# Order of the three product terms inside a k tile: by token half instead of alternating halves

## The chip, the cores and the metric

The kernel runs on one core of one Trainium2 chip. The metric is the device time of one execution in microseconds; the time before is 1610.29 us, the median of three runs (1606.36, 1610.29 and 1698.71).

## The reference

One step of a two-layer decoder trunk in float32 on 576 tokens: a prompt of 512 and 8 x 8 sample tokens, model width 1024. Layer 0 mixes tokens with a chunked gMLP (width 3072), layer 1 with a recurrent block (RG-LRU, width 1024); a SwiGLU block (inner width 2816) follows each, and every block sits between two RMS norms. Nearly all of the arithmetic is in dense products:

```python
def gmlp_mixer(h, ...):
    z = gelu(h @ w_in + b_in); u, v = split(z)
    v = layer_norm(v); mixed = causal product of w_s with v, in chunks of 128
    return (u * mixed) @ w_out, v
def rglru_mixer(h, ...):
    y_br, x_br = split(h @ w_in)
    ... conv, gates, scan over tokens ...
    return (hs * gelu(y_br)) @ w_out
def swiglu(h, w_in, w_out):
    g, u = split(h @ w_in)
    return (silu(g) * u) @ w_out
x = x + rms_norm(mixer(rms_norm(x)));  x = x + rms_norm(swiglu(rms_norm(x)))
```

## The kernel before

Activations lie transposed: features on the 128 partitions, the 576 tokens along the free axis. The tokens are cut into two halves of 288 (HT), so that a half's sums fit one PSUM bank. A unit is one tile of 128 output features: its two halves take banks 2m and 2m+1, the pair m of four pairs.

Each float32 operand is split in two parts of a narrower format: activations into `hh` (high) and `hl` (low), weights into `whi` and `wlo`. A product then takes three matmuls for each k tile (128 input features) and each half: high weights with `hh`, high weights with `hl`, low weights with `hh`. The dropped fourth term is low times low. TensorE therefore runs 6 matmuls of 128 x 288 per k tile and unit, all issued by the helper `mm` (line 455), so every row of these matmuls bears line 455.

The stages, in order: V (the gMLP's v, lines 524 to 580, tokens as output rows, 384 columns wide), U (`u_body`, line 592, 24 units of 8 k tiles, with the chunk mixing between units), and then the phases GO, FI0, FO0, RI, RO, FI1, FO1. The FI phases and RI are units of 8 k tiles (`tile_unit`, line 718) behind an opening part (`first_tiles`, line 667). GO, FO0, RO and FO1 are `out_phase` (line 626): two groups G of 512 output features, each with four pairs open at once and the k tiles in the outer loop.

Two helpers set the order of the six matmuls. `three` (line 457) alternates the halves: bank a, bank b, for each of the three terms. It serves U, RI's and the FI phases' units behind the opening part, and in `out_phase` all k tiles but the last four of each group. `one_half` (line 467) does the three terms of one half, all into one bank. It serves the last four k tiles of each group of `out_phase` (for all of half 0 first, then half 1, lines 648 to 665) and all of `first_tiles`. Over the whole kernel `three` issues 1152 matmuls in U, 480 in each group of GO, 1920 in each FI phase, 432 in each group of FO0 and FO1, 576 in RI and 96 in each group of RO: 8448 in all. `one_half` issues 192 in each of the four out phases and 192 in each of the three opening parts: 1344.

Round TensorE: SP loads weights into four slots of `stage`; ScalarE rounds them to `whi` (line 800), VectorE subtracts to `wlo` (line 1109), and both wait for the unit that used the slot before. ScalarE and VectorE read finished pairs out of PSUM. A unit's only signal, `unit_done`, sits on the last matmul that the last call of `three` returns, the second half's low-weight term; in the last unit of U and of each FI phase every second k tile's last matmul also counts `h_pair_used` up.

Of the kernel before, what the change touches and what calls it, by code (L numbers as in the profile page):

```python
# [38 lines left out]
def trunk_kernel(nc, x_prompt, x_sample, state_conv, state_h, norm_gains,  # L39
# [7 lines left out]
    TT = T + TS  # L47
    HT = TT // 2
# [26 lines left out]
    with ExitStack() as ctx:  # L75
        def sb(name, shape, dt=F32):
            return ctx.enter_context(nc.sbuf_tensor(name, shape, dt))
# [6 lines left out]
        hh = sb("hh", [P, KD, TT], F32R)  # L84
        hl = sb("hl", [P, KD, TT], F32R)
# [34 lines left out]
        ps = ctx.enter_context(nc.psum_tensor("ps", [P, 8, BANK], F32))  # L120
# [18 lines left out]
        def half(h):  # L139
            return slice(h * HT, (h + 1) * HT)  # L140
# [63 lines left out]
        def xc(h):  # L204
            return wide[:, XC0 + h * TT:XC0 + (h + 1) * TT]
# [4 lines left out]
        def wg(mat, h):  # L210
            return wide[:, WG0 + (mat * KD + h) * P:WG0 + (mat * KD + h + 1) * P]
# [137 lines left out]
        def out_bank(b):  # L349
            return ps[0:P if PIECES[b][1] < NC else TS, OUT_BANK[b], :]  # L350
# [102 lines left out]
        def _(pe):  # L453
            def mm(out, w, x, start, stop):
                return pe.matmul(out, w, x, start=start, stop=stop)  # L455

            def three(m, hi_w, lo_w, k, first, last):

                a, b = ps[:, 2 * m, 0:HT], ps[:, 2 * m + 1, 0:HT]
                mm(a, hi_w, hh[:, k, 0:HT], first, False)  # L460
                mm(b, hi_w, hh[:, k, HT:TT], first, False)
                mm(a, hi_w, hl[:, k, 0:HT], False, False)
                mm(b, hi_w, hl[:, k, HT:TT], False, False)
                mm(a, lo_w, hh[:, k, 0:HT], False, last)
                return mm(b, lo_w, hh[:, k, HT:TT], False, last)

            def one_half(m, h, hi_w, lo_w, k, first, last):

                o = ps[:, 2 * m + h, 0:HT]
                mm(o, hi_w, hh[:, k, half(h)], first, False)  # L470
                mm(o, hi_w, hl[:, k, half(h)], False, False)
                return mm(o, lo_w, hh[:, k, half(h)], False, last)
# [34 lines left out]
            for k in range(KD):  # L507
                last = pe.transpose(ps[:, 7, k * TS:(k + 1) * TS], xin[NC][:, k * P:(k + 1) * P], ident[0:TS, 0:TS])
# [56 lines left out]
            for g in range(GRP):  # L565
                at = 4 * BANK + BANK + g * P if g < 4 else 6 * BANK + g * P - 4 * P
                last = pe.transpose(psf[:, at:at + P], wraw[:, g, :], ident[:, :])
# [7 lines left out]
            for k in range(KD):  # L575
                last = pe.transpose(ps[:, 5, 64 + 32 * k:96 + 32 * k], sraw[:, k * P:(k + 1) * P], ident[0:32, 0:32])
# [15 lines left out]
            def u_body(i, first=False, last_body=False):  # L592
                for c in range(6):
                    n = base["U"] + c
                    m = c % 3
                    pe.wait_ge(lo_ready, i * 6 + (n + 1))
                    if first and c < 3:
                        pe.wait_ge(z_evicted, NT * (GRP - 1) + min(2 * c + 2, NT))
                    else:
                        pe.wait_ge(pair_free[m], i * 2 + (c // 3))  # L600
                    for k in range(KD):
                        if last_body and c == 5 and k in (2, 5):
                            mix(i * 6 + 3 + k // 5, k // 5, 1, i * 2 + 1)
                        at = three(m, whi[:, slot(n), k * P:(k + 1) * P], wlo[:, slot(n), k * P:(k + 1) * P],
                                   k, k == 0, k == KD - 1)
                        if last_body and c == 5 and k % 2 and k < KD - 1:
                            at.then_inc(h_pair_used, 1)
                    at.then_inc(unit_done, 1)
                    if first and c < 2 or last_body and c == 5:
                        continue  # L610
                    if c % 3 == 2:

                        pe.wait_ge(ln_done, i * (2 * NT) + (c // 3 + 1) * NT)
                    gshift, f = divmod(c - 2, 3)
                    if first and c == 2:
                        pe.wait_ge(blk_landed, 16 * NB)
                        pe.wait_ge(rb_ready, 1)
                    mix(i * 6 + (c - 2), f, gshift % 2, i * 2 + gshift)
# [7 lines left out]
            def out_phase(name):  # L626
# [8 lines left out]
                for G in range(2):  # L635
                    first = base[name] + G * per
                    for j in range(per - 2):
                        pe.wait_ge(lo_ready, first + j + 1)
                        pe.wait_ge(a_lo, G * per + AB[name] + j + 1)
                        for kk in range(units[j][1]):  # L640
                            for m in range(4):
                                if j == 0 and kk == 0:
                                    pe.wait_ge(pair_free[m], G + free0[name][m])
                                last = three(m, *weights(first + j, kk, m), 2 * (j % 4) + kk, j == 0 and kk == 0, False)
                        last.then_inc(unit_done, 1)
# [72 lines left out]
            def tile_unit(n, m, freed, last_unit, i=0, per=0):  # L718
                pe.wait_ge(lo_ready, i * per + (n + 1))
                pe.wait_ge(pair_free[m], freed)  # L720
                for k in range(KD):
                    last = three(m, whi[:, slot(n), k * P:(k + 1) * P], wlo[:, slot(n), k * P:(k + 1) * P],
                                 k, k == 0, k == KD - 1)
                    if last_unit and k % 2 and k < KD - 1:
                        last.then_inc(h_pair_used, 1)
                last.then_inc(unit_done, 1)
# [21 lines left out]
            for mat in range(2):  # L748
                for h in range(KD):
# [3 lines left out]
                    for b in range(2):  # L753
                        last = mm(ps[:, 2 * (e % 4) + b, 0:HT], wg(mat, h), xc(h)[:, half(b)], True, True)
# [13 lines left out]
            for k in range(KD):  # L768
                last = pe.transpose(ps[0:36, 4 + k // 4, (k % 4) * P:(k % 4 + 1) * P], sout[:, k, :], ident[:, :])
            last.then_inc(so_turned, 1)  # L770
            pe.wait_ge(pair_free[3], free0["END"][3])
            for h in range(2):

                for k in range(KD):
# [7 lines left out]
                    for b, (hf, c) in enumerate(PIECES):  # L782
                        if hf == k // 4 and (c >= 2) == (h == 1):
                            r = P if c < NC else TS
                            last = pe.transpose(out_bank(b)[:, (k % 4) * P:(k % 4 + 1) * P],
                                                xT[:, k, c * P:c * P + r], ident[:, :])
# [916 lines left out]
```

## Time and profile before

| | |
|---|---|
| device time, median of three runs | 1610.29 us (1606.36, 1610.29, 1698.71) |
| span of the profiled execution | 1606.8 us |
| TensorE busy with matmuls | 1564.4 us, 97% of the span, 11250 matmuls |
| VectorE, ScalarE, GpSimd busy | 796.9, 563.7, 302.7 us |
| mean granted TensorE clock | 0.989 of full speed |
| HBM traffic over the span | 82 GB/s |

The profiled execution has no device time listed apart from its span; of the three listed times, one lies just under that span, one 3.5 us above it. A matmul's row is longer than the time to the next row's start, since matmuls are pipelined and their ends are modelled: the pace is read from start to start.

### The profile page before, as it was taken

What the parts mean: (1) busy time and instruction counts of PE and PEld (TensorE: products, weight loads), DVE (VectorE), ACT (ScalarE), POOL (GpSimd) and SP (SyncE); (2) the same over time, 40 slices, a digit from 0 to 9 for tenths busy, and PEclk for the clock granted to TensorE, in tenths of its full rate; (3) what the DMA queues carried; (4) which work ended last, traced back from release to release, by engine and by line L of the source; (5) the groups of instructions that cost most, each with busy time, mean ns of one, the idle gap of its engine ahead of it and who ended that gap; (6) DMA issues with size and microseconds to landing.
All of it is one profiled execution on the core that took longest, in us unless ns stands there. A gap on an engine that the chain in (4) does not pass through costs nothing.

```text
span 1606.8 us, 27610 instructions
## 1 busy us (share of the span) xinstructions
PE 1564.4 (97%) x11250; PEld 1538.5 (96%) x11250; DVE 796.9 (50%) x1033; ACT 563.7 (35%) x786; POOL 302.7 (19%) x260
## 2 busy tenths in 40 slices
PE   7999999999999899999999999997999999999997
PEld 7999999999999899999999989997899999999996
DVE  6444676674444832322353558767663233235444
ACT  5344422224343521212142434474442212124433
POOL 0100033331000412121110015336222121110002
PEclk9999999999999999999999999998999999999998
DMA  6322333322222133223232241122222232223211
GB/s 228 100 79 72 88 95 90 90 84 93 80 90 68 40 92 91 78 78 91 66 105 66 80 118 53 53 80 66 66 66 80 78 91 78 78 79 92 81 51 63
DMA packets 170498, 133.37 MB, mean 83 GB/s; under 512 B 4888, under 2 KB 147504, under 8 KB 170292
## 3 DMA queue, kind: packets, MB, share of 16 engines
q1 hardware_dynamic: 168756, 128.30, 26.6%
q0 software_dynamic: 1664, 3.95, 0.9%
q8 instruction: 58, 0.95, 0.2%
q14 instruction: 20, 0.16, 0.0%
HBM read 128.92 MB, written 3.29 MB: 82 GB/s over the span
## 4 chain that ended last, share of the span: by engine, by line
PE 88%; DVE 5%; POOL 2%; ACT 2%; issue 1%; DMA 0%; SPq 0%; ACTq 0%; POOLq 0%; DVEq 0%
PE ps L455 87%; DVE yb L1370 1%; DVE acc L1126 1%; DVE hl L1157 1%; POOL wide L1644 1%; DVE acc L1136 1%; ACT whi L800 0%; ACT wide L1070 0%; POOL sout L1643 0%; POOL s L1651 0%; DMA wide<-in_x_prompt_dram 0%; PE ps L517 0%; POOL sout L1642 0%; ACT wide L1076 0%; ACT yb L1071 0%
## 5 line engine op out<-in xcount | busy, mean ns | idle before, releaser
L455 PE MATMUL ps<-hh,whi 128*128 128x288 f32 x3264 | 745.3, 299 | 19.9 <-DVE hl L1157 6.7
L455 PE MATMUL ps<-hh,wlo 128*128 128x288 f32 x3264 | 736.8, 296 | 0.0
L455 PE MATMUL ps<-hl,whi 128*128 128x288 f32 x3264 | 736.0, 296 | 0.0
L455 PEld LDWEIGHTS ps<-hh,whi 128*128 128x128 f32 x3264 | 539.8, 189 | 28.5 <-issue 12.6
L455 PEld LDWEIGHTS ps<-hh,wlo 128*128 128x128 f32 x3264 | 540.7, 190 | 0.0
L455 PEld LDWEIGHTS ps<-hl,whi 128*128 128x128 f32 x3264 | 540.2, 190 | 0.5
L1109 DVE TENSOR_TENSOR wlo<-stage,whi 128x1024 fp32r<-128x1024 f32 (+2 forms) x240 | 284.3, 1188 | 317.0 <-ACT whi L800 316.7
L800 ACT ACTIVATE whi<-stage 128x1024 fp32r<-128x1024 f32 (+2 forms) x240 | 240.8, 1017 | 447.9 <-PE ps L455 430.7
L1613 POOL TENSOR_TENSOR wide<-wide,tmp 128x576 f32 x44 | 96.9, 2201 | 443.6 <-DVE tmp L1307 443.6
L1017 ACT ACTIVATE wide<-wide (+1 forms) x44 | 29.9, 685 | 332.5 <-DVE wide L1307 332.4
L1307 DVE TENSOR_TENSOR tmp<-ps,rb 128x576 f32<-128x576 f32 x76 | 57.4, 755 | 175.7 <-PE ps L455 175.7
L1167 DVE TENSOR_TENSOR hl<-wide,hh 128x1152 fp32r<-128x1152 f32 (+1 forms) x80 | 109.3, 1366 | 7.0 <-ACT hh L871 7.0
L1307 DVE TENSOR_TENSOR wide<-ps,rb 128x576 f32 (+1 forms) x44 | 33.1, 757 | 144.0 <-PE ps L455 136.9
L455 PE MATMUL ps<-wlo,hh 128*128 128x384 f32 (+1 forms) x320 | 99.9, 337 | 0.0
L871 ACT ACTIVATE hh<-wide 128x1152 fp32r<-128x1152 f32 (+1 forms) x80 | 88.5, 1107 | 29.5 <-POOL wide L1644 15.1
L1605 POOL TENSOR_TENSOR xT<-xT,yb 128x288 f32<-128x288 f32 x45 | 50.3, 1123 | 243.0 <-DVE yb L1370 243.0
L455 PE MATMUL ps<-whi,hh 128*128 128x384 f32 x264 | 90.4, 342 | 0.0
L455 PE MATMUL ps<-whi,hl 128*128 128x384 f32 x264 | 89.1, 338 | 0.0
L1581 POOL TENSOR_TENSOR wide<-wide,tmp 128x576 f32 (+1 forms) x24 | 53.0, 2210 | 111.3 <-DVE wide L1302 111.3
L455 PEld LDWEIGHTS ps<-wlo,hh 128*128 128x128 f32 (+1 forms) x320 | 56.3, 178 | 0.3
L1136 DVE TENSOR_TENSOR acc<-acc,tmp 128x288 f32<-128x288 f32 x56 | 30.9, 552 | 51.3 <-ACT tmp L846 51.1
L455 PEld LDWEIGHTS ps<-whi,hh 128*128 128x128 f32 x264 | 49.7, 188 | 0.7 <-issue 0.2
(153 smaller groups left out, 911.1 us busy)
## 6 DMA issues: line engine op xcount, KB each, us to landing
stage<-in_ffn_w_in_dram SPq DMA_DIRECT2D x88, 512.0 KB, 3.8
stage<-in_ffn_w_out_dram SPq DMA_DIRECT2D x40, 512.0 KB, 3.8
stage<-in_gm_w_in_dram SPq DMA_DIRECT2D x32, 384.0 KB, 3.6
stage<-in_gm_w_in_dram SPq DMA_DIRECT2D x24, 512.0 KB, 3.8
stage<-in_gm_w_out_dram SPq DMA_DIRECT2D x24, 512.0 KB, 3.8
stage<-in_rg_w_in_dram SPq DMA_DIRECT2D x16, 512.0 KB, 3.9
stage<-in_rg_w_out_dram SPq DMA_DIRECT2D x8, 512.0 KB, 3.7
wide<-in_x_prompt_dram SPq DMA_DIRECT2D x2, 1024.0 KB, 7.4
```

The source lines that it names most:

```text
L455: return pe.matmul(out, w, x, start=start, stop=stop)
L800: act.activation(whi[:, s, 0:width], stage[:, s, 0:width], ACT.Copy).then_inc(hi_ready, 1)
L871: act.activation(hh[:, at:at + nk, :].rearrange("p k n -> p (k n)"), source(name, k, nk), ACT.Copy).then_inc(a_hi, 1)
L1017: act.activation(w, w, ACT.Silu).then_inc(f_act, 1)
L1109: dve.tensor_tensor(wlo[:, s, 0:width], stage[:, s, 0:width], whi[:, s, 0:width].bitcast(F32), ALU.subtract).then_inc(lo_ready, 1)
L1126: dve.tensor_tensor(acc[:, at], acc[:, at], tmp[:, r % 3, at], ALU.add).then_inc(sq_added, 1)
L1136: dve.tensor_tensor(acc[:, half(h)], acc[:, half(h)], tmp[:, r % 3, half(h)], ALU.add).then_inc(psq_added, 1)
L1167: dve.tensor_tensor(hl[:, at:at + nk, :].rearrange("p k n -> p (k n)"), wide[:, src0:src0 + nk * TT], hh[:, at:at + nk, :].rearrange("p k ...
L1307: return dve.tensor_tensor(halves(out), pair(m), halves(rb[:, :]), ALU.mult)
L1581: pool.tensor_tensor(w, w, tmp[:, x % 3, :], ALU.mult).then_inc(gated, 1)
L1605: pool.tensor_tensor(x, x, yt(k)[:, half(h)], ALU.add).then_inc(res_ready, 1)
L1613: pool.tensor_tensor(w, w, tmp[:, c, :], ALU.mult).then_inc(ffn_gated, 1)
```

## The change

Inside `three` the six calls are replaced by two calls of `one_half`. Where the order was half 0, half 1 for each of three terms, it is now three terms of half 0, then three of half 1. The same matmuls, with the same operands and banks, are issued, and what `three` returns is still the last low-weight matmul of half 1.

```diff
             def three(m, hi_w, lo_w, k, first, last):
 
-                a, b = ps[:, 2 * m, 0:HT], ps[:, 2 * m + 1, 0:HT]
-                mm(a, hi_w, hh[:, k, 0:HT], first, False)
-                mm(b, hi_w, hh[:, k, HT:TT], first, False)
-                mm(a, hi_w, hl[:, k, 0:HT], False, False)
-                mm(b, hi_w, hl[:, k, HT:TT], False, False)
-                mm(a, lo_w, hh[:, k, 0:HT], False, last)
-                return mm(b, lo_w, hh[:, k, HT:TT], False, last)
+                one_half(m, 0, hi_w, lo_w, k, first, last)
+                return one_half(m, 1, hi_w, lo_w, k, first, last)
```

TensorE's rows at the start of the loop over FI0's units (line 731 before, 726 after), before; the names are output `ps`, then moving operand and weights, and x2 is one matmul for each half:

```order
L731 UNCONDITIONAL_BRANCH
L731 ISA
L720 REGISTER_ALU
L455 MATMUL ps<-hh,whi 128x288 x2
L455 MATMUL ps<-hl,whi 128x288 x2
L455 MATMUL ps<-hh,wlo 128x288 x2
```

The same place now:

```order
L726 UNCONDITIONAL_BRANCH
L726 ISA
L715 REGISTER_ALU
L455 MATMUL ps<-hh,whi 128x288
L455 MATMUL ps<-hl,whi 128x288
L455 MATMUL ps<-hh,wlo 128x288
L455 MATMUL ps<-hh,whi 128x288
L455 MATMUL ps<-hl,whi 128x288
L455 MATMUL ps<-hh,wlo 128x288
```

One k tile's three pairs have become two runs of three; the second run is half 1. Nothing stands between them.

TensorE's rows at the end of the loop over U's units, before; `wsT` and `wsblk` are the chunk mixing behind the unit:

```order
L455 MATMUL ps<-hh,wlo 128x288 x2
L613 REGISTER_ALU
L585 REGISTER_ALU
L455 ISA
L455 MATMUL ps<-wsT,yb 128x128 x4
L455 ISA
L455 MATMUL ps<-wsblk,yb 128x64
L621 REGISTER_ALU
L621 COMPARE_AND_BRANCH
L455 MATMUL ps<-hh,whi 128x288 x2
```

The same place now:

```order
L455 MATMUL ps<-hl,whi 128x288
L455 MATMUL ps<-hh,wlo 128x288
L608 REGISTER_ALU
L580 REGISTER_ALU
L455 ISA
L455 MATMUL ps<-wsT,yb 128x128 x4
L455 ISA
L455 MATMUL ps<-wsblk,yb 128x64
L616 REGISTER_ALU
L616 COMPARE_AND_BRANCH
L455 MATMUL ps<-hh,whi 128x288
```

The mixing keeps its place behind the unit's last matmul. VectorE, ScalarE, GpSimd and SP have the same rows in the same order as before, but for line numbers.

## Rows read from the trace of the kernel before

**Rows 1.** The page: engines' busy time, and the chain that ended last, by engine.
```profile
PE 1564.4 (97%) x11250; PEld 1538.5 (96%) x11250; DVE 796.9 (50%) x1033; ACT 563.7 (35%) x786; POOL 302.7 (19%) x260
...
PE 88%; DVE 5%; POOL 2%; ACT 2%; issue 1%; DMA 0%; SPq 0%; ACTq 0%; POOLq 0%; DVEq 0%
```

**Rows 2.** Busy time by stretch, all engines: stretch, length, busy (instructions), granted clock, DMA.
```profile
80.00:518.00 438.00, 438.00 (x3102) 430.52 (x3100) 243.43 (x346) 156.34 (x202) 63.77 (x44) 1.00 0.28 85
...
559.00:952.00 393.00, 392.88 (x2959) 392.85 (x2960) 143.75 (x145) 113.35 (x139) 49.75 (x31) 1.00 0.30 87
...
1041.00:1115.00 74.00, 65.00 (x458) 64.03 (x457) 48.61 (x43) 42.41 (x52) 42.10 (x52) 0.93 0.21 65
...
1190.00:1589.00 399.00, 396.61 (x2987) 396.24 (x2986) 146.60 (x153) 114.47 (x146) 50.72 (x25) 1.00 0.26 75
```

**Rows 3.** Waits, longest first in total: who waited for whom, us, times, longest.
```profile
ACT whi L800 <- PE ps L455: 430.7, 110, 6.2
```

**Rows 4.** Groups of instructions by line and shape, the 128 x 288 matmuls and their loads.
```profile
L455 PE MATMUL ps<-hh,whi 128*128 128x288 f32 x3264 | 745.3, 299 | 19.9 <-DVE hl L1157 6.7 <-DVE hl L1167 4.1 <-issue 3.7
L455 PE MATMUL ps<-hh,wlo 128*128 128x288 f32 x3264 | 736.8, 296 | 0.0
...
L455 PEld LDWEIGHTS ps<-hl,whi 128*128 128x128 f32 x3264 | 540.2, 190 | 0.5
```

**Rows 5.** Line 455 alone by stretch: PE busy (matmuls), PEld busy (loads), clock, DMA.
```profile
368.80:432.40 63.60, 63.60 (x480) 63.60 (x479) 1.00 0.29 92
445.30:507.50 62.20, 62.20 (x480) 62.20 (x480) 1.00 0.31 94
559.50:872.50 313.00, 313.00 (x2350) 313.00 (x2349) 1.00 0.28 84
885.60:941.60 56.00, 56.00 (x433) 56.00 (x433) 1.00 0.33 93
1190.60:1503.60 313.00, 313.00 (x2350) 313.00 (x2349) 1.00 0.29 84
1516.80:1572.60 55.80, 55.80 (x431) 55.80 (x431) 1.00 0.19 57
```

**Rows 6.** Timeline of PE in U's loop: start, duration, matmuls merged.
```profile
249.68 0.42 PE L455 MATMUL ps<-hh,whi 128*128 128x288 f32 x2
...
251.28 0.42 PE L455 MATMUL ps<-hh,whi 128*128 128x288 f32 x2
```

**Rows 7.** Timeline of PE, GO's first group, its end: `one_half`, half 0 then 1.
```profile
432.52 0.29 PE L455 MATMUL ps<-hh,whi 128*128 128x288 f32 x1
...
438.84 0.30 PE L455 MATMUL ps<-hh,whi 128*128 128x288 f32 x1
```

**Rows 8.** Timeline of PE, GO's second group: `three`, then `one_half` from 507.65.
```profile
445.25 0.42 PE L455 MATMUL ps<-hh,whi 128*128 128x288 f32 x2
445.51 0.42 PE L455 MATMUL ps<-hl,whi 128*128 128x288 f32 x2
445.77 0.42 PE L455 MATMUL ps<-hh,wlo 128*128 128x288 f32 x2
446.03 0.42 PE L455 MATMUL ps<-hh,whi 128*128 128x288 f32 x2
...
507.65 0.29 PE L455 MATMUL ps<-hh,whi 128*128 128x288 f32 x1
...
515.57 0.59 PE L455 MATMUL ps<-ones,acc 128*96 128x1 f32 x6
```

**Rows 9.** Timeline of PE, FI0's opening part: half 0 to 539.48, half 1 behind.
```profile
533.16 0.29 PE L455 MATMUL ps<-hh,whi 128*128 128x288 f32 x1
...
539.48 0.29 PE L455 MATMUL ps<-hh,whi 128*128 128x288 f32 x1
...
547.08 0.29 PE L455 MATMUL ps<-hh,whi 128*128 128x288 f32 x1
```

## Prediction

> **What bounds the kernel now.** I read the page's busy times and its chain of waits first. TensorE is busy for 97% of the span and holds 88% of the chain that ended last [rows 1]; no other engine is busy for more than half of it. The table by stretch says where that is so: in the long stretches 80 to 518, 559 to 952 and 1190 to 1589 TensorE is busy from end to end at the full granted clock, while VectorE and ScalarE have time to spare [rows 2]. The list of waits agrees: ScalarE's rounding of weights waited 430.7 us in all for TensorE's matmuls [rows 3], so the supply runs ahead and is held back by TensorE. Only in 1041 to 1115, RI's gates and scan, does TensorE idle, 65.00 us busy of 74.00 [rows 2]. In the long stretches each nanosecond more or less from one matmul's start to the next goes straight into the time.
>
> The change touches nothing else. All 8448 matmuls of `three` stay, with their operands, banks and signals; the signal of a unit is still on the last matmul of half 1, so no engine is woken earlier. No wait is added or removed, no queue is passed. Half 0 of a pair is finished three matmuls before half 1 instead of one, but nobody is told: both halves are read out behind the same signal. What can differ is the pace alone, from start to start, of the same matmuls in another order.
>
> **The pace of the old order.** The rows of the matmuls have modelled ends (mean 296 to 299 ns, [rows 4]), so I take starts. A matmul's row is some 0.29 us long at a spacing of 0.13, so at each edge of a stretch it counts one matmul too many, two in all. In FI0's units with FO0's first group, 313.00 us / (2350 - 2) = 133.3 ns; FI1's the same; GO's first group 63.60 / 478 = 133.1 [rows 5]. In U's loop 12 matmuls take 251.28 - 249.68 = 1.60 us, 133.3 each [rows 6]. But the second groups of GO, FO0 and FO1 run faster: 62.20 / 478 = 130.1, 56.00 / 431 = 129.9, 55.80 / 429 = 130.1 [rows 5], and from 445.25 to 507.65 exactly 480 matmuls give 130.0 [rows 8]. The code and the order are those of the first group. So the same order has two steady paces, 133.3 and 130.0, and the faster one is entered straight out of a stretch of `one_half` without a stop. Stretches at 130.0: 480 + 432 + 432 = 1344 matmuls. The rest, 8448 - 1344 = 7104, I take at 133.3, RI and RO by their neighbours. Sum before: 1344 x 130.0 + 7104 x 133.3 = 174.7 + 947.0 = 1121.7 us.
>
> **The pace of the new order.** It already runs in this kernel, as `one_half`. At the end of GO's first group, half 0: 48 matmuls from 432.52 to 438.84, 131.7 ns each [rows 7]; half 1: 48 from there to 445.25, 133.5 each [rows 7, 8]. At the end of GO's second group 60 matmuls (48 of half 0, 12 of half 1) take 515.57 - 507.65 = 7.92 us, 132.0 each [rows 8]. In FI0's opening part half 0 runs 48 matmuls from 533.16 to 539.48, 131.7 each, and half 1 57 from 539.48 to 547.08, 133.3 each [rows 9]; there the bank changes after every three matmuls in half 1, as it will in the new order. So a half-0 run costs 131.7, a half-1 run 133.4, and running three matmuls in a row into one bank costs nothing that these rows show. What they do not show is a change of half after every three. I bound it by the slowest and fastest steady pace of any 288-column stretch, 133.5 and 130.0, and take the mean of the two halves, 132.5, as the nearest rows are these.
>
> **The sum.** 8448 x 132.5 = 1119.4 us, against 1121.7: 2.3 us less. A part of RI's units lies where TensorE waits for others; at 0.8 ns for each of a few hundred matmuls that is under 0.3 us. The profiled span of 1606.8 would become 1604.5. The median of the runs stands 3.5 us above that span, and I carry the difference over to it: 1610.3 - 2.3 = 1608.0 us. Two of the three listed runs lie 3.9 us apart, so this change is smaller than the scatter, and 2% (32 us, about what a measurement of this kernel can tell from no change) would take 32 / 8448 = 3.8 ns on every matmul, more than the whole distance between the fastest and slowest pace seen.
>
> **A rule that speaks against the change.** In the old order four matmuls in a row use the same high weights, in the new never more than two. The table by shape has one weight load for each matmul, 3264 in each group and 11250 in all [rows 1, 4], and in GO's second group the pair starts are 0.26 us apart where the weights stay (445.25 to 445.51) and where they change (445.51 to 445.77) alike [rows 8]. The Trainium skill, TensorE: Matmul & The Clock Gate, section "Step-by-step: what each phase is for", says that weights usually stay put over many matmuls, so that one load can serve a run of them. By that rule the old order would need two loads for six matmuls and the new one four; the trace disagrees, since the loads are repeated already and keep their pace. It is the third rival below.
>
> **The rivals.** First, the fast pace becomes the rule: the new order locks into 130.0 everywhere, as the second groups did behind `one_half`. 8448 x 130.0 = 1098.2, 23.5 us less, 1587 us. For it: the pace is there for 62 us on end. Against: no stretch of `one_half` itself runs at it. I give it 0.09, and some way toward it is in the range.
>
> Second, slower: the change of half becomes a price of its own. The slow pace of the old order is 4 x 3.3 = 13 ns more for every four matmuls than the fast one. If that extra is tied to the return to another half and bank rather than to elapsed time, the new order pays it once in three: 130.0 + 13.3 / 3 = 134.4 ns, 8448 x 134.4 = 1135.4, 13.7 us more, 1624 us. It decides from the point where every run of three ends in a step of over 140 ns. For it: half 1 is slower than half 0 in [rows 7 to 9], so the address of the half matters somehow. Against: the old order changes the half at every matmul and yet holds 130.0 for 480 of them. Chance 0.12.
>
> Third, the change of weights costs. The equal pair spacings above bound it by the resolution of the rows, 10 ns; two more changes for each of 1408 k tiles would be 28 us, 1638 us. Against it: `one_half` has as many changes as the new order and runs at 132.5 all the same. Chance 0.03.
>
> Fourth, nothing at all changes, because TensorE were not the limit: 1610 us. The long stretches without an idle moment speak against it, and it would not be told from the forecast. It is counted with it.
>
> **How the numbers follow.** The forecast has 0.74: from all matmuls at half 0's pace (8448 x 131.7 = 1112.6, 1601 us) to all at half 1's (133.4: 1127.0, 1616 us), with the runs' scatter 1598 to 1619. The remaining 0.02 are causes I don't see. The range 1588 to 1623 takes in nearly all of the forecast and about half of the first two rivals. Faster than 1578 would need 128.9 ns on every matmul, below any steady pace: 0.04. Slower than 1642 needs the third rival at its full price or an unknown one: 0.06. Within 2%: 0.90.
>
> **What would show it.** Right: FI0's loop in the new profile runs between 131.7 and 133.4 ns from start to start, the three second groups no longer stand out at 130.0 (they lose 1344 x 2.5 ns = 3.4 us), the slow stretches gain 7104 x 0.8 = 5.7 us, and VectorE, ScalarE and GpSimd keep their busy times. Wrong: a pace under 131 or over 134 in FI0's loop, long steps at each change of half, new idle time in front of matmuls, or a granted clock other than full in the long stretches.

## The result and the profile after

The changed kernel takes 1612.35 us (median of 7 runs, 1610.45 to 1613.63) against 1609.47 us for the kernel before (median of 7). Runs over 1.5% above the fastest of their kernel (1698.71 us here, one of 1631.11 us further down) were in a slow state and are left out of the ratios; without it the median before is 1607.9 us. The ratio is 1.0024, 95% interval 1.0015 to 1.0033: slower by about a quarter of a per cent, some 4 us, where 1608.0 us, 2.3 us faster than the 1610.29 known then, had been forecast. The time lies inside the range and far inside 2%, but the sign is wrong, and the interval is narrow enough to say so.

The page of the kernel after, span and first lines of its parts 1 and 4:

```profile
span 1609.2 us, 27610 instructions
...
PE 1567.8 (97%) x11250; PEld 1541.6 (96%) x11250; DVE 797.7 (50%) x1033; ACT 563.4 (35%) x786; POOL 303.3 (19%) x260
...
PE 88%; DVE 5%; POOL 2%; ACT 2%; issue 1%; DMA 0%; SPq 0%; ACTq 0%; POOLq 0%; DVEq 0%
```

Beside [rows 1] this is the same picture: the same counts, the other engines' busy times within a microsecond, TensorE busy for 3.4 us more. The span grew by 2.4 us. The chain that ended last tells best where, since it merges TensorE's long stretches. Its pieces in the kernel before (start, length, what):

```profile
80.13 437.75 PE ps L455 x3096
...
559.12 392.83 PE ps L455 x2958
...
1114.78 34.20 PE ps L455 x246
...
1190.23 393.29 PE ps L455 x2960
```

The same pieces after:

```profile
80.04 439.25 PE ps L455 x3096
...
560.24 394.27 PE ps L455 x2958
...
1117.61 32.66 PE ps L455 x246
1191.36 394.74 PE ps L455 x2960
```

The counts are equal, so the differences are pace: +1.50, +1.44 and +1.45 us in the three long stretches, each of which holds one of the fast second groups (GO, FO0, FO1), and -1.54 us in the last part of RO (1114.78 before, 1117.61 after). Together that is 2.85 us of the span's 2.4; the rest lies in shorter pieces. The table of line 455 by stretch after, to be read as [rows 5]: stretch, length, PE busy (matmuls), PEld busy (loads), clock, DMA:

```profile
369.50:432.50 63.00, 63.00 (x475) 63.00 (x474) 1.00 0.30 92
446.50:508.50 62.00, 62.00 (x467) 62.00 (x466) 1.00 0.31 94
562.50:872.50 310.00, 310.00 (x2328) 310.00 (x2327) 1.00 0.29 85
889.50:943.50 54.00, 54.00 (x407) 54.00 (x407) 1.00 0.33 95
1193.50:1503.50 310.00, 310.00 (x2327) 310.00 (x2327) 1.00 0.29 85
1522.50:1576.50 54.00, 54.00 (x407) 54.00 (x406) 1.00 0.18 58
```

With two matmuls taken off each count for the edges, as in the prediction, GO's second group is at 62.00 / 465 = 133.3 ns, those of FO0 and FO1 at 54.00 / 405 = 133.3, and FI0 with FO0's first group at 310.00 / 2326 = 133.3. The loops have not moved; the three groups that ran at 130.0 now have the loops' pace. 1344 matmuls x 3.3 ns = 4.4 us, which is the three differences of the chain. The timeline of PE in FI0's loop shows the steps:

```profile
715.96 0.29 PE L455 MATMUL ps<-hh,whi 128*128 128x288 f32 x1
716.09 0.29 PE L455 MATMUL ps<-hl,whi 128*128 128x288 f32 x1
716.22 0.29 PE L455 MATMUL ps<-hh,wlo 128*128 128x288 f32 x1
716.36 0.30 PE L455 MATMUL ps<-hh,whi 128*128 128x288 f32 x1
716.49 0.29 PE L455 MATMUL ps<-hl,whi 128*128 128x288 f32 x1
```

Every start is 0.13 to 0.14 us after the last, also where the half changes (716.22 to 716.36). The view prints hundredths of a microsecond, too coarse for a price of 2 or 3 ns; the trace keeps the starts in whole nanoseconds. From 563 to 773 us all 1574 steps are 133 or 134 ns, at changes of half as elsewhere: there is no price there, not even a small one. In the kernel before the same window has the same mean, but of other steps: three of 130 to 132 ns, then one of 140. So the equal 133.3 of the loops before and after does not say that one cause sets both.

The 1.54 us that RO gave back are the clock's. The table by stretch for the first 4 us of that piece of the chain, in the kernel before (all engines; the third figure from the end is the granted clock):

```profile
1114.78:1118.90 4.12, 4.12 (x20) 4.12 (x21) 4.12 (x4) 3.65 (x7) 0.00 (x0) 0.59 0.42 123
```

and after:

```profile
1117.61:1122.00 4.39, 4.39 (x33) 4.39 (x34) 4.39 (x4) 4.39 (x10) 0.00 (x0) 1.00 0.43 120
```

Behind RI, where TensorE idles between waits [rows 2], the clock falls to its lower level of 1.2 GHz for a time. In the trace before, this still covered 1115.4 to 1118.9 us, and some 14 matmuls took 240 ns instead of 133, 1.5 us in all. In the trace after it covered 1112.2 to 1115.6 us, ahead of a wait of RO for VectorE, and the piece behind that wait ran at full clock. The slowed matmuls of the trace before are of the first group's last four k tiles, whose order the change leaves alone. The same piece takes 33.90 us in a second trace of the kernel before and 34.21 and 32.67 us in the first two experiments below; of these two the one that alternates in RO's first group has the short time. So the order inside RO's first group does not decide it. Whether the change does so by shifting RO against the clock is not shown, and the 1.5 us are not put down to it.

### The profile page after: what moved, and what is told of

Read it like the earlier page. It is cut to its first block, busy times and chain, and to the rows that moved or that the text cites. A ratio compares the mean times of both kernels' runs of the same rounds, so it can differ in the third digit from the quotient of the medians.

```text
span 1609.2 us, 27610 instructions
## 1 busy us (share of the span) xinstructions
PE 1567.8 (97%) x11250; PEld 1541.6 (96%) x11250; DVE 797.7 (50%) x1033; ACT 563.4 (35%) x786; POOL 303.3 (19%) x260
## 4 chain that ended last, share of the span: by engine, by line
PE 88%; DVE 5%; POOL 2%; ACT 2%; issue 1%; DMA 0%; SPq 0%; ACTq 0%; POOLq 0%; DVEq 0%
PE ps L455 87%; DVE yb L1365 1%; DVE acc L1121 1%; DVE hl L1152 1%; POOL wide L1639 1%; DVE acc L1131 1%; ACT whi L795 0%; ACT wide L1065 0%; POOL sout L1638 0%; POOL s L1646 0%; DMA wide<-in_x_prompt_dram 0%; PE ps L512 0%; POOL sout L1637 0%; ACT wide L1071 0%; ACT yb L1066 0%
## 5 line engine op out<-in xcount | busy, mean ns | idle before, releaser
L455 PE MATMUL ps<-hh,whi 128*128 128x288 f32 x3264 | 977.2, 299 | 18.9 <-DVE hl L1152 6.7
L455 PE MATMUL ps<-hl,whi 128*128 128x288 f32 x3264 | 965.2, 296 | 0.0
L455 PE MATMUL ps<-hh,wlo 128*128 128x288 f32 x3264 | 963.3, 295 | 0.0
L455 PEld LDWEIGHTS ps<-hh,whi 128*128 128x128 f32 x3264 | 615.1, 188 | 27.4 <-issue 11.0
L455 PEld LDWEIGHTS ps<-hh,wlo 128*128 128x128 f32 x3264 | 617.9, 189 | 0.0
L455 PEld LDWEIGHTS ps<-hl,whi 128*128 128x128 f32 x3264 | 616.0, 189 | 0.5
L795 ACT ACTIVATE whi<-stage 128x1024 fp32r<-128x1024 f32 (+2 forms) x240 | 240.9, 1018 | 451.1 <-PE ps L455 434.3
```

The costliest lines, as they stand in the source:

```text
L795: act.activation(whi[:, s, 0:width], stage[:, s, 0:width], ACT.Copy).then_inc(hi_ready, 1)
```

## The experiments

Paces below are a stretch of the table of line 455, its length over its count less two; one matmul in the count is 0.3 ns in a stretch of 60 us, under 0.1 ns in one of 200 us, 0.7 ns in one of 24 us and 1.5 ns in one of 12 us. "Over" means above columns / 2.4, one column for each clock at 2.4 GHz: 120.0 ns for 288. The kernel before ran beside every group of experiments. In code and rows, `...` stands for lines left out.

**The second groups alone keep the old order.**

```diff
+            three = halves_in_turn
...
-                                last = three(m, *weights(first + j, kk, m), ...)
+                                last = (alternating if G else three)(m, *weights(first + j, kk, m), ...)
```

> The new order everywhere but in the second groups of the four out phases, which alternate as before. Theory A (the loss is the second groups of GO, FO0 and FO1 alone, where the old order ran at 130.0 ns and the new one at 133.3): these groups run at 130.0 again, the rest stays at 133.3, and the time is that of the kernel before within 1 us. Rival B (the new order is slower everywhere by some tenths of a nanosecond): 1 to 2 us above the kernel before, with the second groups fast. Rival C (the fast pace also needs the alternating order in the stretch ahead of it): the second groups run at 133.3, and the time is that of the changed kernel, some 3 us above.

Here `halves_in_turn` is the new order and `alternating` the old one. Measured: 1613.03 us against 1607.71, ratio 1.0033 (1.0020 to 1.0046). GO's second group and FI0's loop:

```profile
448.00:508.00 60.00, 60.00 (x453) 60.00 (x452) 1.00 0.32 95
563.00:813.00 250.00, 250.00 (x1878) 250.00 (x1877) 1.00 0.28 82
```

60.00 / 451 = 133.0 and 250.00 / 1876 = 133.3. Rival C holds: alternating is not enough for the fast pace, what runs ahead of the stretch counts too. And it is not only the `one_half` just ahead, whose order is that of the kernel before.

**The second groups alone get the new order.**

```diff
-                                last = three(m, *weights(first + j, kk, m), ...)
+                                last = (halves_in_turn if G else three)(m, *weights(first + j, kk, m), ...)
```

> The new order in the second groups of the out phases alone. Theory A: the three fast groups go from 130.0 to 133.3 ns, 1344 matmuls x 3.3 ns = 4.5 us more at most, so 2.5 to 4.5 us above the kernel before. Rival B: no more than 1344 of 8448 of the loss, under 0.6 us above.

Measured: 1612.74 us against 1607.71, ratio 1.0035 (1.0022 to 1.0048), 5.0 us or 3.5 to 7.7 by the interval, where theory A wanted 2.5 to 4.5. GO's second group and FO0's:

```profile
448.00:508.00 60.00, 60.00 (x452) 60.00 (x451) 1.00 0.32 97
...
892.00:942.00 50.00, 50.00 (x377) 50.00 (x377) 1.00 0.30 88
```

60.00 / 450 and 50.00 / 375 are both 133.3 ns. The new order in one sixth of its matmuls brings the whole loss. That settles where the loss is; the other 7104 matmuls keep their 133.3 in either order. The 5.0 us lie above theory A's upper end, but the interval takes in the 4.4 us of the chain.

**The first k tile of each unit by halves, the rest alternating.**

```diff
             def three(m, hi_w, lo_w, k, first, last):
+                if first:
+                    one_half(m, 0, hi_w, lo_w, k, first, last)
+                    return one_half(m, 1, hi_w, lo_w, k, first, last)
                 a, b = ps[:, 2 * m, 0:HT], ps[:, 2 * m + 1, 0:HT]
```

> The first k tile of every unit and of every out-phase group runs by halves, all others alternate. Theory D (a stretch of alternating matmuls entered from one by halves takes up the 130.0 ns pace): the long loops of FI0 and FI1 fall to 130 to 131 ns after the first k tile of each unit, up to 7000 x 3 ns = 20 us below the kernel before. Rival E (the entry alone is not enough: what counts is on which matmul of a cycle of four the stretch is entered): the loops stay at 133.3, the time within 2 us of the kernel before, some stretches fast and others not.

Measured: 1609.86 us against 1607.71, ratio 1.0015 (1.0007 to 1.0024). GO's second group and FI0's loop:

```profile
448.00:508.00 60.00, 60.00 (x453) 60.00 (x452) 1.00 0.30 93
563.00:813.00 250.00, 250.00 (x1885) 250.00 (x1885) 1.00 0.28 82
```

FI0 comes to 250.00 / 1883 = 132.8, a little faster; GO's second group loses its 130.0 (60.00 / 451 = 133.0). Theory D fails: an entry from a stretch by halves does not give the fast pace as such. Rival E is right in that, but its own forecast is not met either: the loops are not at 133.3, and no stretch is at 130.0. Why the loops are half a nanosecond faster is not known.

**The halves in the order 0 1, 1 0, 0 1**, run twice, the second time for its trace.

```diff
                 mm(b, hi_w, hh[:, k, HT:TT], first, False)
-                mm(a, hi_w, hl[:, k, 0:HT], False, False)
                 mm(b, hi_w, hl[:, k, HT:TT], False, False)
+                mm(a, hi_w, hl[:, k, 0:HT], False, False)
```

> The halves in the order 0 1, 1 0, 0 1 for the three terms of each k tile: two matmuls in a row into one bank once in six. Theory F (the 133.3 ns are a floor that any regular order comes to, and 130.0 a state that only strict alternation can hold): 133.3 everywhere, the time as the changed kernel's, some 3 us above the kernel before. Rival G (the pace is the sum of prices of single steps, 128 ns from half 0 to half 1 and 132 back): between 129 and 133, and below the kernel before by several us.

> The order 0 1, 1 0, 0 1 once more, for its trace, which had FI0's loop at 136.8 and FI1's at 131.7 ns though both run the same instructions. Theory L: FI0 again near 137, FI1 near 132. Rival M: each of the loops at either pace.

Measured: 1603.1 us, ratio 0.9979 (0.9961 to 0.9997), but its times spread over 1599.79 to 1616.32 us, with one at 1631.11, while the kernel before spread over 5 us beside it. FI0's and FI1's loops in the first trace:

```profile
575.00:825.00 250.00, 250.00 (x1816) 250.00 (x1815) 1.00 0.27 78
...
1205.00:1455.00 250.00, 250.00 (x1901) 250.00 (x1900) 1.00 0.29 84
```

and in the second:

```profile
575.00:825.00 250.00, 250.00 (x1877) 250.00 (x1876) 1.00 0.28 82
...
1205.00:1455.00 250.00, 250.00 (x1877) 250.00 (x1877) 1.00 0.28 82
```

The same instructions at full clock: 250.00 / 1814 = 137.8 ns and 250.00 / 1899 = 131.6 in one execution, 133.3 and 133.3 in the other (one time, 1609.24 us). Neither F nor G, nor L: for this order rival M holds, a stretch draws its pace anew in each execution and keeps it to its end. The two traces are from two chips, but the spread of the twelve times, and the two paces inside one trace, are from one.

**The kernel before once more**, for its trace.

> The kernel before once more, for its trace. Theory L (what pace a stretch takes is fixed by how it is entered, and the kernel before always enters the same way): second groups of GO, FO0 and FO1 at 130.0, all else at 133.3 as in the first trace. Rival M (it is drawn anew in each execution): other stretches are the fast ones.

Measured: one time, 1609.75 us (1607.51 beside it). GO's second group, and the middle of RO's second group:

```profile
448.00:508.00 60.00, 60.00 (x464) 60.00 (x463) 1.00 0.33 97
...
1128.00:1140.00 12.00, 12.00 (x95) 12.00 (x94) 1.00 0.46 132
```

GO's second group is at 60.00 / 462 = 129.9 again, and the loops are at 133.3. RO's second group has 93 matmuls in 12 us, 129.0 by the count and 130.0 by the starts; the first trace had 90, 133.3. So in these two traces L holds for the long stretches of the kernel before, and M for the short one behind RI's waits.

**Half 1 ahead of half 0.**

```diff
-                one_half(m, 0, hi_w, lo_w, k, first, last)
-                return one_half(m, 1, hi_w, lo_w, k, first, last)
+                one_half(m, 1, hi_w, lo_w, k, first, last)
+                return one_half(m, 0, hi_w, lo_w, k, first, last)
```

> By halves as in the changed kernel, but half 1 ahead of half 0 in each k tile. Theory H (the pace is one steady state of three matmuls into one bank, whichever half): FI0's and FI1's loops at 133.3 ns again, no stretch at 130. Rival I (the addresses of a half set the pace): a pace other than 133.3 by a nanosecond or more.

Measured: 1612.82 us (one run; the kernel before 1607.51 beside it). FI0's loop has 1577 matmuls in 210 us, FI1's 1465 in 195 us: 133.3 ns both, as theory H has it. It does not separate the address from the change of half, since both halves still take turns.

**256 columns instead of 288.**

```diff
+            def narrow_alternating(m, hi_w, lo_w, k, first, last):
+                n = HT if first else 256
+                for w, x in ((hi_w, hh), (hi_w, hl), (lo_w, hh)):
+                    for h in range(2):
+                        at = mm(ps[:, 2 * m + h, 0:n], w, x[:, k, h * HT:h * HT + n], ...)
...
             out_phase("RO")
+            order.append(narrow_by_half)
             ffn_in("FI1")
```

> All matmuls of the alternating k tiles but the first of each unit have 256 columns instead of 288 (32 tokens of each half are left out of the sums); up to RO they alternate, from FI1 on they go by halves. Theory J (the matmuls' columns set the pace): 32 / 2.4 = 13 ns less, FI0's loop at 118 to 120 ns. Rival K (something that is there once for each matmul, its weight load or its issue, sets the 133.3): FI0 and FI1 within 3 ns of 133. If FI0 and FI1 differ by over 2 ns, the order matters more where columns count less.

Measured: 1509.02 us (one run; 1607.51 beside it). FI0's loop (alternating) and FI1's (by halves):

```profile
563.00:773.00 210.00, 210.00 (x1749) 210.00 (x1748) 1.00 0.31 90
1205.00:1400.00 195.00, 195.00 (x1625) 195.00 (x1624) 1.00 0.31 92
```

120.2 and 120.1 ns: between 288 and 256 columns the columns set the pace (theory J), one weight load for each matmul notwithstanding. With a first k tile of 288 in each eight, the mean is 260 columns, 108.3 ns at 2.4 GHz, and 12 ns come on top, much as at 288 (120.0 and 10.0 to 13.3). At the lower clock, in the result's stretch of RO, the steps are 240 ns, just 288 / 1.2: a column for each clock and nothing on top. So at full clock the pace is read here as columns / 2.4 plus a part of 10 to 13 ns, and only this part is in dispute.

**Both runs of three read the same half.**

```diff
-                one_half(m, 0, hi_w, lo_w, k, first, last)
-                return one_half(m, 1, hi_w, lo_w, k, first, last)
+                return order[-1](m, hi_w, lo_w, k, first, last)
...
+            def early(m, hi_w, lo_w, k, first, last):
+                for h, at in enumerate((0, 0)):
+                    for i, (w, x) in enumerate(terms(hi_w, lo_w)):
+                        r = mm(ps[:, 2 * m + h, 0:HT], w, x[:, k, at:at + HT], ...)
...
+            def late(m, hi_w, lo_w, k, first, last):
+                for h, at in enumerate((HT, HT)):
...
```

> By halves, but both of a k tile's runs of three read the same tokens: up to RO both read half 0 (half 1's tokens are left out), from FI1 on both read half 1 (half 0's are left out). The banks still change after every three. Theory N (it is where half 1 begins in hh and hl that keeps the new order at 133.3): FI0's loop and FO0 at 131.7 ns, FI1's loop and FO1 at 133.3. Rival O (the change of bank after three, or the run of three itself, sets 133.3): 133.3 in all of them.

Measured: 1603.8 us (one run; 1607.73 beside it). FI0's loop (half 0 twice) and FI1's (half 1 twice):

```profile
563.00:773.00 210.00, 210.00 (x1597) 210.00 (x1596) 1.00 0.30 87
1205.00:1400.00 195.00, 195.00 (x1465) 195.00 (x1464) 1.00 0.28 81
```

210.00 / 1595 = 131.7 and 195.00 / 1463 = 133.3, as theory N says. The banks change after three in both, so it is not the bank, and not the run of three.

**Half 1's slice from token 256.** The edit is against the run above; from FI1 on the same two slices alternate.

```diff
-                for h, at in enumerate((0, 0)):
+                for h, at in enumerate((0, 256)):
```

> Half 1's runs read 288 tokens from token 256 on instead of 288 (tokens 544 to 575 are left out, 256 to 287 are taken twice); up to RO by halves, from FI1 on alternating. Theory N with the beginning of the slice as what counts (token 256 lies 1024 bytes into the tile, token 288 lies 1152): FI0's loop at 131.7 instead of 133.3, and FI1's loop at 131.7 or 130.0. Rival P (any change of the moving slice costs the same): FI0's and FI1's loops at 133.3 as in the changed kernel.

Measured: 1601.84 us (one run; 1607.73 beside it). FI0's loop (by halves) and FI1's (alternating):

```profile
563.00:773.00 210.00, 210.00 (x1597) 210.00 (x1596) 1.00 0.30 86
1205.00:1400.00 195.00, 195.00 (x1483) 195.00 (x1483) 1.00 0.29 83
```

131.7 in both, 195.00 / 1481 in the second. Moving a slice by 32 tokens takes 1.7 ns off the mean of all matmuls, in either order. Tokens 256 to 287 are read twice here, so this run alone does not say that it is the beginning.

**A cut of 256 and 320 tokens**, alternating and part by part.

```diff
+            SPLIT = (slice(0, 256), slice(256, TT))
+            def uneven(m, hi_w, lo_w, k, first, last):
+                for i, (w, x) in enumerate(((hi_w, hh), (hi_w, hl), (lo_w, hh))):
+                    for cols in SPLIT:
+                        last_mm = mm(split_out(m, cols), w, x[:, k, cols], ...)
```

> Nothing is left out here: in U's units and in the loops of FI0 and FI1 the 576 tokens are cut in 256 and 320 instead of 288 and 288, alternating as in the kernel before; the two parts lie side by side over the pair's two banks, and VectorE reads them as one run of 576. Everything else is the kernel before. Theory N with the beginning of the slice: the mean pace in U and in FI0's and FI1's loops falls from 133.3 to 131.7 ns, 4992 matmuls x 1.67 ns = 8.3 us below the kernel before. Rival R (the gain in the shifted run came from the tokens read twice, not from where the slice begins): 133.3, and the time of the kernel before within 2 us.

> The same cut of 256 and 320 tokens, with the three terms of the first part ahead of those of the second, as in the changed kernel; out phases and RI alternate as in the kernel before. Theory N: with both slices beginning well, the order no longer matters, mean pace 131.7 ns and the time of the alternating version within 1 us, 8 us below the kernel before. Rival S (by halves costs something of its own beside the beginning of the slice): above the alternating version by 2 us or more.

Measured: 1607.14 us, ratio 0.9991 (0.9982 to 1.0000), and 1606.84 us, ratio 0.9993 (0.9984 to 1.0002). In the first, GO's first group (288 and 288, as before) and FI0's loop (256 and 320):

```profile
370.00:430.00 60.00, 60.00 (x452) 60.00 (x451) 1.00 0.29 89
563.00:773.00 210.00, 210.00 (x1577) 210.00 (x1576) 1.00 0.29 85
```

133.3 in the mean in both; the second kernel, which swaps the two loops of the edit, has the same count in FI0, and S (2 us more for it) is out. Theory N with the beginning alone fails here. The result is what rival R wanted, so R is not answered by this pair: either reading twice had helped, or the widths count. The next runs ask which.

**Seven beginnings.**

```diff
+            SLICE = {'U': (16, 288), 'GO': (32, 288), 'FI0': (64, 288), 'FO0': (8, 288), 'RI': (128, 288), 'FI1': (48, 288), 'FO1': (160, 288)}
...
+                at, n = SLICE[stage_now[-1]]
...
+                for h in range(2):
+                    for i, (w, x) in enumerate(((hi_w, hh), (hi_w, hl), (lo_w, hh))):
+                        r = mm(ps[:, 2 * m + h, 0:n], w, x[:, k, at:at + n], ...)
```

> By halves, and both runs of three read the same 288 tokens, which begin at another token in each stage: U 16, GO 32, FI0 64, FO0 8, RI 128, FI1 48, FO1 160 (the other tokens are left out of these sums; k tiles lie 576 tokens apart). Theory N (the beginning counts, and beginnings at multiples of 64 tokens, as half 0's in every k tile, are the good ones): FI0 and RI at 131.7 ns, U, GO, FO0, FI1 and FO1 at 133.3 or so. Rival T (half 1 is slow because its slice ends at the end of the k tile's 576): 131.7 in all.

Measured: 1607.43 us (one run; 1605.80 beside it). FI0 (64), RI (128) and FI1 (48):

```profile
563.00:813.00 250.00, 250.00 (x1900) 250.00 (x1900) 1.00 0.29 84
...
996.00:1020.00 24.00, 24.00 (x184) 24.00 (x183) 1.00 0.32 91
1210.00:1450.00 240.00, 240.00 (x1802) 240.00 (x1802) 1.00 0.27 81
```

250.00 / 1898 = 131.7, 24.00 / 182 = 131.9 and 240.00 / 1800 = 133.3. GO (32), FO0 (8) and FO1 (160) come to 133.0 to 133.3 as well; U is cut into short pieces by the mixing and is not read. Theory N holds: with 288 columns, the beginnings at multiples of 64 tokens give 131.7, the others 133.3. Rival T is out, since no slice here ends with the k tile and four go at 133.3 all the same. So is R: every stage reads its tokens twice, and only two are faster.

**Seven widths from token 0.**

```diff
+            SLICE = {'U': (0, 256), 'GO': (0, 272), 'FI0': (0, 280), 'FO0': (0, 264), 'RI': (0, 240), 'FI1': (0, 320), 'FO1': (0, 224)}
```

> By halves, both runs of three read from token 0, with another number of columns in each stage: U 256, GO 272, FI0 280, FO0 264, RI 240, FI1 320, FO1 224 (the other tokens are left out; the first k tile of each unit keeps 288 or more). If the beginning alone counts, the pace is columns / 2.4 plus the 11.7 ns that half 0 shows at 288: 118.3, 125.0, 128.3, 121.7, 111.7, 145.0 and 105.0 ns. If the width counts too, the part above columns / 2.4 differs among them by a nanosecond or more, and is over 13 ns at 320 or 256, where the uneven cut was slow.

Measured: 1577.61 us (one run; 1605.80 beside it). FI0 (280), FO0 (264), FI1 (320) and FO1 (224):

```profile
550.00:790.00 240.00, 240.00 (x1873) 240.00 (x1872) 1.00 0.28 83
795.00:840.00 45.00, 45.00 (x377) 45.00 (x376) 1.00 0.30 99
...
1160.00:1430.00 270.00, 270.00 (x1843) 270.00 (x1843) 1.00 0.25 74
1455.00:1485.00 30.00, 30.00 (x266) 30.00 (x265) 1.00 0.26 80
```

264 columns: 45.00 / 375 = 120.0, 10.0 ns over. 280 (281 in the mean, as one k tile in eight has 288): 240.00 / 1871 = 128.3, 11.2 over. 320: 270.00 / 1841 = 146.7, 13.3 over, though it begins at token 0. 224: 30.00 / 264 = 113.6, 20.3 over, so at this width the columns no longer set the pace; what does was not followed. The width counts, then. That the uneven cut lost by its widths what it had won by its beginning fits, but is not shown for each part: in the second uneven kernel's FI0 loop the steps of 256 columns take 119.1 ns in the mean and those of 320 take 147.6, 12.4 and 14.2 over, both more than the 11.7 that 288 columns from a multiple of 64 take.

**Rows of 640 positions, half 1 from 320**, by halves and alternating; everything is computed. U and GO keep the old rows.

```diff
+        HP = 320
...
+        hhp, hlp = (t[:, :].rearrange("p (k h n) -> p k h n", k=KD, h=2) for t in (hhs, hls))
...
+            def act_of(low, k, h):
+                if padded[-1]:
+                    return (hlp if low else hhp)[:, k, h, 0:HT]
+                return (hl if low else hh)[:, k, half(h)]
...
             out_phase("GO")
+            padded.append(True)
             ffn_in("FI0")
```

> Nothing is left out. From FI0 on, hh and hl have rows of 640 positions, half 0 from 0 and half 1 from 320, so every slice begins at a multiple of 64; V, U and GO keep the old rows. By halves. Theory N: FI0, FO0, RI, RO, FI1 and FO1 at 131.7 ns, the end of each out phase at 131.7 in half 1 too, U and GO at 133.3. Against the changed kernel 6336 x 1.67 + 576 x 1.67 = 11.5 us less, some 8 us below the kernel before. Rival U (the place helps only where both runs read the same slice): 133.3, the changed kernel's time.

> The same rows of 640, with the alternating order of the kernel before. Theory N: FI0, RI and FI1 at 131.7 ns or below, 8 us below the kernel before; the second groups of FO0 and FO1 between 130.0 and 131.7, so within 2 us of the run by halves. Rival V (alternating keeps its 133.3 unless entered luckily): FI0 and FI1 at 133.3, the time of the kernel before.

Measured by halves: 1601.81 us (1601.70 to 1602.27) against 1607.96, ratio 0.9962 (0.9950 to 0.9974). GO's first group (old rows), then FI0, FO0's second group and FI1, all matmuls of PE:

```profile
370.00:430.00 60.00, 60.00 (x452) 1.00 0.29 89
...
563.00:773.00 210.00, 210.00 (x1597) 1.00 0.29 85
...
890.00:940.00 50.00, 50.00 (x382) 1.00 0.34 96
...
1205.00:1400.00 195.00, 195.00 (x1483) 1.00 0.29 83
```

133.3, then 131.7, 50.00 / 380 = 131.6 and 131.7. Alternating: 1602.77 us, ratio 0.9965 (0.9951 to 0.9979). GO's second group (old rows) and FO0's (new rows):

```profile
450.00:505.00 55.00, 55.00 (x425) 1.00 0.31 95
...
890.00:940.00 50.00, 50.00 (x382) 1.00 0.32 92
```

55.00 / 423 = 130.0 in the old rows, 131.6 in the new; FI0 and FI1 are at 131.7 there too. Theory N carries over, with no token read twice, rivals U and V are out, and both orders run alike in the new rows. Both beat the kernel before and the changed one: by 6.2 and 5.2 us against the kernel before, a little less than the 8 expected.

## Why the prediction was right or wrong

What bounds the kernel was right: TensorE's pace from start to start. ScalarE's wait for TensorE (434.3 us in all against 430.7), the other engines' busy times and the chain are much those of before, and the differences of the chain's long pieces are accounted for by pace and clock.

The pace of the old order was right. 133.3 and 130.0 came back in a second trace of the kernel before, and when the new order was put into the second groups alone, they carried the whole loss.

The step that failed is the last of "The pace of the new order": "take the mean of the two halves, 132.5, as the nearest rows are these". The mean does not apply. The rows were read rightly: half 0's runs take 131.7 and half 1's 133.4 [rows 7 to 9]. But where the two take turns after every three matmuls, all of them go at the slower pace: every step read in FI0's loop is 133 or 134 ns with half 0 and half 1 in turn, and the mean is 133.3 with half 1 alone and 131.7 with half 0 alone. With half 1's beginning moved to position 320 and nothing left out, both go at 131.7. With 133.3 in place of 132.5 the sum reads 8448 x 133.3 = 1126.1 against 1121.7, 4.4 us more, and the three long stretches of the chain measured +1.50 + 1.44 + 1.45 = 4.4. The text had this case as one end of the forecast (all at half 1's pace, 1616 us) and gave it no weight of its own. So FI0's loop lies inside the 131.7 to 133.4 that was named as the sign of being right; what failed is the gain of 5.7 us in the slow stretches, which was nothing, while the loss in the second groups was 4.4 us instead of 3.4. RO's clock gave 1.5 us back in the profiled execution.

The sentence that was nearest to the cause stood under the second rival: "half 1 is slower than half 0, so the address of the half matters somehow". It was used as an argument for a price at each change of half. The trace after has no such price, and moving the place where half 1 begins (to 256 or 320) takes the pace to 131.7 with every change of half left in place.

The rivals: the fast pace as the rule did not come, and the new order took 130.0 at 288 columns in no stretch of any trace. The change of half as a price (134.4 ns) did not come. A price for the change of weights did not come: by halves, with its four changes in six, the padded kernel runs at the same 131.7 ns as alternating, with two. The Trainium skill, TensorE: Matmul & The Clock Gate, section "Step-by-step: what each phase is for", says that weights typically stay put across many matmuls, so that they are loaded once. The trace disagrees for this kernel, where every matmul has its own load (11250 of each), as the prediction said.

The size of the change was about right, under a third of one per cent and far from 2% on either side; its direction was not.

Open: why the alternating order can hold 130.0 at all behind the second groups' entry, and what in that entry decides it. That it hangs on what runs ahead is shown (the runs with the second groups alternating behind a first group by halves, and with the first k tile by halves, both lost it). That the order 0 1, 1 0, 0 1 and RO's short second group draw their pace anew in each execution is shown too. The mechanism is not, and neither is why a beginning at a multiple of 64 should matter.

## What to carry to other kernels

When a matmul stream without gaps sets the time, read its pace from start to start in every stretch where the same shape runs, and treat each as a state of its own: two paces seen apart need not average when their operands take turns; here the slower one ruled. A pace that differs between two stretches with equal instructions but other addresses is worth one run that swaps the address alone; here 32 positions of padding behind each half gave 6 us where the order of the terms cost 4. And a loss that sits in a few stretches is found fastest by putting the change there alone; run the rest alone as well, which here lost just as much (5.3 us), since what runs ahead of those stretches counts too.

## What the runs showed of the hardware

At 288 columns and full clock the time from one matmul to the next took a few steady values, 130.0, 131.7, 133.3 and once 137.8 ns, and kept one through a whole stretch of up to 2352 matmuls; only the loops of the kernel with the first k tile by halves had a mean between them, 132.8. Above columns / 2.4 GHz that is 10.0, 11.7, 13.3 and 17.8 ns, with a weight load in front of every matmul. At the lower clock the same matmuls took 240 ns, 288 / 1.2, with nothing on top.

By halves, slices of 288 that begin at a multiple of 64 float32 positions (0, 64, 128, 256, 320) took 131.7 ns when all matmuls of the stretch began so; those at 8, 32, 48, 160 and 288 took 133.3. Alternating, 0 with 256 and 0 with 320 took 131.7 as well. A bad beginning does not bar a fast pace in every order: with half 1 from 288, the alternating order ran at 130.0 in the second groups, and a loop in the order 0 1, 1 0, 0 1 at 131.7 in one execution. The part above the columns' own time also depends on the width: 10.0 ns at 264 columns, 13.3 at 320, 20.3 at 224, all from position 0.

The order 0 1, 1 0, 0 1 ran at 137.8 ns in one execution and at 133.3 in another, in the same loop: a change that looks faster by its median can owe that to the draw.
